# x, residual and output stored block by block; weight conversions in half rows; x ahead of the conditioning weights; weight folding moved away from the gMLP scratch

## What is computed

```python
for l in range(DEPTH):                            # DEPTH = 2
    mod = adaln(c, w_mod[l], b_mod[l])            # 9 x (shift, scale, gate) from SiLU(c) @ w_mod
    mod_c = adaln(c_ctx, w_mod[l], b_mod[l])
    h = ffn_sublayer(h, mod, 0, norm_g[l, 0], ffn_w_gu[l, 0], ffn_w_down[l, 0])
    hc = ffn_sublayer(hc, mod_c, 0, ...)
    xa_c, ga_c, u_c, v_c, f_c = mix_in(hc, mod_c, norm_g[l, 1], w_in[l])
    y_lru_c, state_c = lru_branch(xa_c, ...)      # bidirectional gated scan; context first
    xa, ga, u, v, f = mix_in(h, mod, norm_g[l, 1], w_in[l])
    y_lru, _ = lru_branch(xa, ..., state_c)
    h = mix_out(h, mod, y_lru, ga, u, v, f, gmlp_ws[l], gmlp_bs[l], w_out[l])
    h = ffn_sublayer(h, mod, 6, norm_g[l, 2], ffn_w_gu[l, 1], ffn_w_down[l, 1])
    ...                                           # the same for hc, except in the last layer
return rmsnorm(h, final_norm_g)
```

## Time and profile before

| | |
|---|---|
| median of 3 runs (all) | 5353.59 us (5323.27, 5353.59, 5664.02) |
| profiled execution: time / span of its slowest core | 5341.42 us / 5339.9 us |
| spans of the 8 cores | 5308.5 to 5339.9 us |
| PE busy | 4829.8 us, 90% |
| DVE, ACT, POOL busy | 40%, 30%, 20% |
| granted PE clock, mean | 0.961 to 0.964 of full speed |
| moved by DMA | 893 MB, 167 GB/s |
| plain DMAs (q1) / converting DMAs (q0), share of the 16 DMA engines | 45.9% / 15.0% |

### The profile page before, as it was taken

The page is one execution under the profiler, slowest core; times in us unless marked ns, Lnnn a source line. Parts: engine busy times, 40 slices in busy tenths (PEclk is TensorE's granted clock), DMA queues, the critical chain, the costliest instruction groups (busy, mean ns, idle before and its releaser), DMA issues.

```text
span 5339.9 us, 84731 instructions; the slowest of 8 cores (5308.5 to 5339.9 us)
## 1 busy us (share of the span) xinstructions
PE 4829.8 (90%) x29137; PEld 2772.7 (52%) x29137; DVE 2116.0 (40%) x3151; ACT 1624.3 (30%) x2551; POOL 1062.5 (20%) x943
## 2 busy tenths in 40 slices
PE   4987889999867999989999989999997679999998
PEld 2553556564424565555546546566544235555554
DVE  2325354544453424323222354434445443534422
ACT  2223333423344212212112243433334432322312
POOL 1311121312111211212121220312210131221210
PEclk9998999999988999999999999999998889999999
DMA  8973668786636667577576646556456444444434
GB/s 179 204 176 113 167 177 214 171 197 184 201 130 170 173 180 205 153 179 171 158 209 160 180 139 185 159 155 175 152 177 211 155 134 144 153 132 152 154 114 150
DMA packets 321601, 893.15 MB, mean 167 GB/s; under 512 B 32032, under 2 KB 83616, under 8 KB 320032
## 3 DMA queue, kind: packets, MB, share of 16 engines
q1 hardware_dynamic: 292960, 767.91, 45.9%
q0 software_dynamic: 28224, 119.82, 15.0%
HBM read 861.37 MB, written 204.24 MB: 200 GB/s over the span
## 4 chain that ended last, share of the span: by engine, by line
PE 74%; DMA 8%; DVE 7%; ACT 4%; issue 4%; POOL 2%; SPq 1%; DVEq 0%; ACTq 0%; POOLq 0%
PE ps L937 42%; PE ps L987 19%; PE ps L1545 4%; PE ps L1030 4%; DMA arena<-wgu_s 2%; PE ps L1052 2%; DMA hT<-arena 1%; DVE arena L1277 1%; DVE arena L1273 1%; DVE arena L1281 1%; DVE arena L994 1%; POOL arena L847 1%; DMA arena<-smalls 1%; DVE arena L890 1%; ACT arena L1248 1%
## 5 line engine op out<-in xcount | busy, mean ns | idle before, releaser
L937 PE MATMUL ps<-arena 128*128 128x384 bf16 (+2 forms) x15136 | 2613.5, 334 | 98.7 <-DMA arena<-wgu_s 40.6
L937 PEld LDWEIGHTS ps<-arena 128*128 128x128 bf16 x15136 | 1480.0, 98 | 1185.7 <-issue 137.2
L987 PE MATMUL ps<-arena 128*128 128x384 bf16 (+2 forms) x7568 | 1346.2, 340 | 2.8 <-DVE arena L948 1.1
L948 DVE TENSOR_TENSOR arena<-arena,ps 128x384 bf16<-128x384 bf16 (+2 forms) x946 | 533.5, 568 | 1837.5 <-PE ps L937 1457.8
L987 PEld LDWEIGHTS ps<-arena 128*128 128x128 bf16 x7568 | 753.6, 100 | 569.3 <-issue 57.5
L946 ACT ACTIVATE arena<-ps 128x384 bf16<-128x384 f32 (+2 forms) x946 | 468.9, 500 | 1541.6 <-PE ps L937 1461.9
L847 POOL TENSOR_TENSOR arena<-arena 128x768 f32<-128x768 f32 (+2 forms) x287 | 503.8, 1755 | 2139.4 <-ACT arena L845 2031.7
L845 ACT ACTIVATE arena<-arena 128x768 f32<-128x768 f32 (+1 forms) x287 | 228.2, 795 | 878.3 <-DVE arena L994 516.9
L994 DVE SCALAR_TENSOR_TENSOR arena<-ps,arena 128x384 f32<-128x384 f32 (+2 forms) x344 | 216.1, 630 | 701.7 <-PE ps L987 532.4
L897 POOL TENSOR_SCALAR arena<-arena 128x768 bf16<-128x768 f32 (+2 forms) x252 | 273.0, 1084 | 898.0 <-DVE arena L890 894.0
L890 DVE TENSOR_TENSOR arena<-arena 128x768 f32<-128x768 f32 (+2 forms) x296 | 292.8, 995 | 71.9 <-POOL arena L897 42.7
(11 more groups left out here) (117 smaller groups left out, 2374.0 us busy)
## 6 DMA issues: line engine op xcount, KB each, us to landing
arena<-wgu_s SPq DMA_DIRECT2D x506, 512.0 KB, 4.9
arena<-wdn_s SPq DMA_DIRECT2D x368, 352.0 KB, 3.3
arena<-wmod_h POOLq DMA_DIRECT2D x72, 512.0 KB, 8.2
hT<-arena SPq DMA_DIRECT2D x24, 1536.0 KB, 11.1
arena<-hT SPq DMA_DIRECT2D x24, 1536.0 KB, 14.0
arena<-win_s SPq DMA_DIRECT2D x66, 512.0 KB, 5.4
wgu_s<-wgu_h POOLq DMA_DIRECT2D x66, 512.0 KB, 11.2
arena<-xc_d SPq DMA_DIRECT2D x64, 384.0 KB, 4.9
```

Source lines behind the costliest of these rows:

```text
L937: ins = e.matmul(ps[:, 0:n], ap[:, kc * 256 + u * 128:kc * 256 + u * 128 + 128], NT[nx][:, kc, off:off + n], start=(kc == 0), stop=(kc == ...
L948: P.op("dve", lambda e: e.tensor_tensor(hid[:, j, off:off + n], sg[q][:, 0:n], PS[banks[1]][:, 0:n], ALU.mult), reads=[R_sg[q], R_ps[banks ...
L987: ins = e.matmul(ps[:, 0:n], ap[:, jj * 128:jj * 128 + 128], hid[:, j, off:off + n], start=(j == 0), stop=(j == JC - 1))
```

## The change

Five things change.

- **Layout.** `xT`, `ctxT`, `hT` and `outTb` were [chunk, partition, token]: one block's row of one chunk is a run of 2 or 3 KB. They become flat arrays in which a block is [partition, chunk, token] (`blocked`), so that a half block of 768 tokens is one run of 12 KB per partition, on the SBUF side too. Blocks of 512 tokens and the context (held in slots of 768) keep runs of 2 KB and 1 KB in SBUF. The first block of x is still loaded chunk by chunk.
- **Start.** The load of `mod` tile 0 waits until chunk 5 of x has landed. All 8 `pos_add`/`sq_pe` steps come first, then `rstd_from`, then the 8 `mod` tiles.
- **Conversions.** A `precast` is issued as two half rows: the leading dimension of both sides is 2, where the built program had 16 pieces of 16384 elements (`wgu`, `win`) or 128 rows of 1408 (`wdn`).
- **Statistics.** `stat_step` goes from 0.08 to 0.16 of the first list, the normalisation from 0.2 to 0.24.
- **Folding and CLc.** `fold_out(0)` goes from the third block's pump to the first block's list; `fold_in(1)` and `fold_out(1)` go to the head of the second sweep's pump. The load of `CLc` is issued before `mix_xa` instead of with the context's Fourier step.

```diff
@@ -416,9 +416,16 @@
...
     CS_d = din("CS", [128, 256], BF16)
-    outT = nc.dram_tensor("outTb", [KC, 128, L], F32, kind="ExternalOutput").ap()
-
-    hT = dscr("hT", [KC, 128, NTOK], F32)
+    outB = nc.dram_tensor("outTb", [D * L], F32, kind="ExternalOutput").ap()
+
+    hB = dscr("hB", [D * L], F32)
+    hBc = dscr("hBc", [D * CTX], F32)
+
+    def blocked(t, tok, n):
+
+        a = D * tok
+        return t[a:a + D * n].rearrange("(p m t) -> p m t", p=128, m=KC)
+
     xc_d = dscr("xc_d", [4, 128, NTOK], F32)
@@ -621,7 +628,7 @@
...
             if k == "mod":
-                P.dma("pool", ap, wmod_h[key[1], key[2]], writes=[res], key=res.name)
+                P.dma("pool", ap, wmod_h[key[1], key[2]], reads=([R_h[0][KC - 3]] if t == 0 else []), writes=[res], key=res.name)
             elif k == "c0":
@@ -654,7 +661,8 @@
...
             st["pc"] = (i + 1) % 4
-            P.dma("pool", s, f, writes=[scr(key), R_pc[i]], key=f"pc{i}")
+            P.dma("pool", s.rearrange("p (a b) -> a p b", a=2), f.rearrange("p (a b) -> a p b", a=2),
+                  writes=[scr(key), R_pc[i]], key=f"pc{i}")
@@ -792,12 +800,11 @@
...
                     if src == "x":
-                        ap = ctxT[m0:m1] if s == 1 else xT[m0:m1, :, tok - CTX:tok - CTX + n]
-                        rd = []
+                        t, rd = (ctxB if s == 1 else xB), []
                     else:
-                        ap = hT[m0:m1, :, tok:tok + n]
-                        rd = [R_hT[k] for k in blocks_of(tok, n)]
-                    P.dma("sp", h[slot][:, m0:m1, off:off + n], ap.rearrange("m p t -> p m t"), reads=rd,
+                        t, rd = (hBc if s == 1 else hB), [R_hT[k] for k in blocks_of(tok, n)]
+                    ap = blocked(t, tok - CTX * (1 - s), n)[:, m0:m1, :]
+                    P.dma("sp", h[slot][:, m0:m1, off:off + n], ap, reads=rd,
                           writes=R_h[slot][m0:m1], key=f"hl{slot}{m0}", group=grp)
@@ -808,13 +815,13 @@
...
                         continue
-                    o = P.dma("sp", outT[m0:m1, :, tok - CTX:tok - CTX + n].rearrange("m p t -> p m t"),
-                              h[slot][:, m0:m1, off:off + n], reads=R_h[slot][m0:m1], key=f"os{slot}")
+                    o = P.dma("sp", blocked(outB, tok - CTX, n)[:, m0:m1, :], h[slot][:, m0:m1, off:off + n],
+                              reads=R_h[slot][m0:m1], key=f"os{slot}{m0}")
                     out_stores.append(o)
...
                     continue
-                P.dma("sp", hT[m0:m1, :, tok:tok + n].rearrange("m p t -> p m t"), h[slot][:, m0:m1, off:off + n],
+                P.dma("sp", blocked(hBc if s == 1 else hB, tok - CTX * (1 - s), n)[:, m0:m1, :], h[slot][:, m0:m1, off:off + n],
                       reads=R_h[slot][m0:m1], writes=[R_hT[k] for k in blocks_of(tok, n)], key=f"hs{slot}{m0}", group=grp)
@@ -1480,8 +1487,10 @@
...
+            def tables():
+                P.dma("sp", clc[0], CLc_d, writes=[R_tm], key="clc")
+
             def prep():
-                P.dma("sp", clc[0], CLc_d, writes=[R_tm], key="clc")
                 P.op("dve", lambda e: e.memset(tmp[0][:, 0:256], 0.0), writes=[R_tmp[0]])
@@ -1510,7 +1519,7 @@
...
                 P.dma("sp", ybf[j, :, 0:256], yb[q][:, 0:256], reads=[R_yb[q]], writes=[R_ybf["c"]], key=f"ybs{q}", group="c")
-            return [lambda: (prep(), run(0), run(1))]
+            return [tables, lambda: (prep(), run(0), run(1))]
@@ -1607,11 +1616,12 @@
...
         banks0 = [nb(), nb()]
-        for t in range(8):
-            mods[t]()
+        for t in range(KC):
             pos_add(sb0, 0, t)
...
         rstd_from(sb0, banks0)
+        for t in range(8):
+            mods[t]()
         n1 = 0
@@ -1639,7 +1649,7 @@
...
                 if l == 0 and i == 2:
-                    slow_bg += mod_steps(0, 5, 6) + [lambda: fold_in(1), lambda: fold_out(0), lambda: fold_out(1)]
+                    slow_bg += mod_steps(0, 5, 6)
                     slow_bg += [lambda t=t: precast_wo(0, t) for t in range(4)] + mod_steps(0, 6, 9) + precast_ffn(1)
@@ -1649,8 +1659,8 @@
...
                     late = l == 0 and i == 1
-                    bg1 = [(0.08, lambda: stat_step(prev))]
-                    bg1 += spread(norm_steps(prev, pslot, l, 1, n2, "mix")[1:], 0.72 if late else 0.2, 0.9 if late else 0.8)
+                    bg1 = [(0.16, lambda: stat_step(prev))]
+                    bg1 += spread(norm_steps(prev, pslot, l, 1, n2, "mix")[1:], 0.72 if late else 0.24, 0.9 if late else 0.8)
                     if i == 1:
@@ -1661,6 +1671,9 @@
...
                     rest = mix_rest(prev, l, n2)
+                    cf = ctx_fourier(prev)
+                    if late:
+                        cf[0]()
                     for u in mix_xa(prev, l, n2):
@@ -1669,7 +1682,7 @@
...
                     if l == 0 and prev["ctx"]:
-                        bg2 += [(0.05, ctx_fourier(prev)[0])]
+                        bg2 += [(0.0, cf[1])]
                     if not is_last:
@@ -1697,7 +1710,7 @@
...
                 if l == 0 and i == 0:
-                    bg2 += spread(mod_steps(0, 2, 3), 0.5, 0.95)
+                    bg2 += spread(mod_steps(0, 2, 3) + [lambda: fold_out(0)], 0.5, 0.95)
                 run(units, bg2)
@@ -1801,7 +1814,7 @@
...
                 if l == 0 and i == 0:
-                    slow_bg += mod_steps(1, 0, 9)
+                    slow_bg += [lambda: fold_in(1), lambda: fold_out(1)] + mod_steps(1, 0, 9)
                     slow_bg += [lambda t=t: precast(("wi", 1, t)) for t in range(6)] + precast_ffn(2)
```

16 lines of the change are left out of this document (11 added, 5 removed).

## The result

The change makes the kernel slower. The changed kernel takes 5455.3 us (median of 4 runs, 5451.55 to 5544.52), the kernel before 5342.6 us (median of 4 runs); the ratio is 1.0225 with a 95% interval of 1.0185 to 1.0265, so 2.25% are lost, 113 us between the medians. Predicted were 5285 us with a range of 5230 to 5400: even its upper end is 55 us too low.

What follows compares the result with a forecast made beforehand. The prediction took PE to bound the kernel, except for DMA at the start and in a few short collisions. Its terms, -20 - 7 - 8 - 9 - 15 = -59 us, took 5341.4 to 5282, said as 5285; range 5230 to 5400.

Steps and rivals of the forecast that it cites:

- What bounds the kernel: Whole kernel: PE bounds it, busy 90% of the span, except for DMA at the start and a few short collisions.
- Layout and half rows: Bursts of conversions: halved packets and longer residual runs let SP's queue move more bytes; -15 us, bounds 0 and -25.
- rival a: Conversions spread over few DMA engines, POOL late and PE behind it at the projection: 5380 to 5415 us, chance 0.12.
- The start: Before the first matmuls: PE starts at 60 instead of 86.25 us; -20 us, bounds -8 and -26.
- Folding: gMLP steps: PE's 9.6 us wait for ACT's copies goes once folds move; -8 us, bounds -10 and +6.
- CLc: Table load issued before the projection, whose matmuls cover its landing: PE's 6.9 us wait goes; -7 us, bounds -7 and 0.
- statistics: First-sweep stages: PE waits less for POOL's sum of squares, 28.2 us before; -9 us, bounds 0 and -20.
- The sum: Whole kernel: -20 - 7 - 8 - 9 - 15 = -59 us from 5341.4 gives 5282, said as 5285.
- rival (b): The start gives little and the collisions stay, DMA-bound as far as 300 us: -25 us, 5316, chance 0.23.
- The signs: Right if PE's wgu_s waits fall below 25 us; wrong if wgu_h waits exceed 15 us or the clock drops below 0.96.
- The chances: Whole kernel's time: 0.15 for faster by over 2%, 0.04 for slower by over 2%, 0.81 for within 2%.

Runs made afterwards that it cites:

- e1: The changed kernel with only the conversions undone, each again one DMA of 16 pieces or of 128 rows of 1408: ratio to before 1.000, 5342.8 us profiled.
- e4: The changed kernel with each conversion issued as two DMAs of 128 half rows: ratio to before 0.998, 5331.5 us profiled.
- e6: e4 with all three folds back in the third block's pump, where they were before: 5296.8 us profiled, ratio to before 0.9947 (0.9887 to 1.0007).
- e14: The changed kernel with the folds back in the third block and the conversions as before, in full rows: 5318.1 us profiled, no ratio.
- e12: The kernel before with the blocked layout of x, residual and output alone: ratio to before 1.0009, 5363.3 us profiled.
- e7: The kernel before with only the start changed: ratio to before 0.9968 (0.9931 to 1.0005), 5319.8 us profiled.
- e5: e4 with each of the two folds at the head of the second sweep cut into two pump steps: ratio to before 0.9949, 5310.9 us profiled.
- e9: The changed kernel with conversions as two DMAs of 128 half rows and each fold in two steps back in the third block: 5327.0 us profiled, no ratio.
- e3: The changed kernel with conversions in whole rows, still with a leading dimension of 2: lowest time 5480.5 us, core median +138 us against before, no ratio.
- e11: The changed kernel with conversions in whole rows and a leading dimension of 8 (8 x 16 x 2048): ratio to before 0.997.
- e10: The changed kernel with conversions of leading dimension 16 in short pieces (16 x 128 x 128 for wgu): ratio to before 1.0158, 5438.1 us profiled.
- e13: The changed kernel with wgu or win conversions as 16 x 64 x 256 and half wdn tiles as 16 x 8 x 1408: ratio to before 0.9985.

## Why the prediction was wrong, point by point

- **What bounds the kernel: right, but one view short.** PE is the bound, and DMA is at the start. I read SP's queue only by landing times. Its waits would have shown that SP already stood 26.4 and 6.2 us for conversions: the conversions are consumed by SP's loads soon after they are issued, so that a longer landing goes straight into the queue that all weights come through.
- **Layout and half rows, -15 us (bounds 0 and -25): the step that failed.** It counted the bytes and lengths of packets, and took no effect at all as its worst case; that a conversion could land later, and that SP's loads wait for it, is not in the term. With the leading dimension at 2 the term is about +115 us (core medians: after +113, e1 -3). The unknown was written down (rival a) and left out of the term. "Halving" the packets is also not what the edit did to a `wgu` tile: its pieces went from 16384 elements to 1024. As for the mechanism which the step did argue, that shorter rows let SP's queue through, the runs with a spread conversion agree: -6 to -11 us (e4 against e1) and -21 us (e6 against e14). The layout's share of it was nothing (e12). And the 40.6 us of which 15 were to be won were those of the core with the longest waits; others had 22.5.
- **Rival (a), 0.12, 5380 to 5415 us: right in the cause, wrong in the place and the price.** Landing 22 to 45 us was said, 31.5 measured, above the threshold of 28. But I let POOL be late with the normalisation, and wrote of the burst at 2288 that POOL's idle time until 2380 "hides even 11 us each". POOL's idle time hides nothing, since it is SP that waits for the landing. Just that stage lost most. POOL's late normalisation did not show: PE's waits at L1037 for L904 are 4.1 us. And "the burst then presses less on SP's loads" was true and worthless: a tile's load in the burst landed in 17.5 us instead of 40.1, well inside my sign of "under 25 us", while PE's waits for tiles went from 40.6 to 113.5 us, because landing is counted from the issue, and the issue was what came late.
- **The start, -20 us: right by itself as far as the runs tell** (e7: core median -16, lag -22 at the end), with the first L944 at 64.8 us on core 7, inside 56 to 66, though the hand-over was 4.8 us later than my 60. The eight tiles follow each other by 2.6 to 4.3 us, where I took 3.2, and the last is used at 49.2 instead of 44 to 45; most of PE's 26.8 us for `wmod_h` are waits for these tiles. What failed was that idle DMA time between 86 and 300 us takes up `woutf` and its stores: 12 us were lost at 204 us (e6 against e4), and 4.5 to 9.0 of them are PE behind ACT, which waits for the fold's own store. The term had priced the bytes of those stores and not this wait.
- **Folding, -8 us (-10 and +6): wrong in sign.** It is about +35 us (e4 against e6). That "six PSUM banks cover for two units of about 2.6 us" makes room for some 5 us of waiting for a store; ACT waited 22.3 us for it in the second sweep and 15.9 us in the first block.
- **CLc, -7 us, and statistics, -9 us: right as waits.** The 6.9 us are gone (2.8 us for DVE stand at the same matmuls now), and 28.2 became 15.9 us. That the time fell by as much is not shown, as neither ran alone; together with the layout, on top of the start, they bring 5 us (core medians: e7 -16, e14 -21).
- **The sum.** Start, CLc and statistics add up to -40 us by the waits that went; measured together with full-row conversions and old folds they are -21 (e14). Some of the gain is given back to waits for `wgu_s` tiles, 36 to 41 us there where e7 has 24 to 39. With the folds moved it is about 0 (e1). So the forecast of 5285 us would have failed with a sound form of the conversions too (e4: 5331.5 us profiled): rival (b), -25 us, is nearest to e14, and the folds take the rest.
- **The signs.** PE's waits for `wgu_s` (75.3 us) did not fall below 25. The wait for `wgu_h` tiles between 100 and 200 us was 3.1 us, under the 15 named. The granted clock did fall below the 0.96 of before, to 0.95, and came with the longer waits of PE; which part of the time is its own no run separates.
- **The chances.** 0.04 for slower by over 2% was far too small. That no transfer before had such a dimension was known, and a landing three times as long was written down; a price for it had to be carried to every consumer, SP's loads first.

## What to carry to other kernels

Where a DMA's shape is changed, look first at its outermost dimension, and keep it at 8 or more: here 2 made landing three times as long at the same share of the engines' time, and 8 did not (what lies between was not run). Follow a late transfer to the queue that waits for it, by that queue's own waits; a short landing time says nothing of a load that could not be issued. A step moved off one stall takes the stall with it if its halves share one scratch and wait for each other's store. Splitting the step into halves with other work between them took the wait away here (e5, e9).

## What the hardware showed that was not expected

- **Packets that carry nothing.** e3 has 107520 packets under 512 bytes more than e1 (139552 against 32032) and 0.43 MB more on its converting queue (120.25 against 119.82): 4.0 bytes each. After has 215040 more and 0.86 MB: 4.0 bytes again. Per row of a conversion (120 conversions of 256 or 128 rows) that makes 7 with a leading dimension of 2; with 8 it is 1 (e11: 15360), with 16 none. That is 16 divided by the leading dimension, less one. What they are the traces don't say. They cost little of the engines' time (15.1% in after, 15.0% before).
- **POOL's issue** of a conversion took 0.5 us before, 1.1 us with 2048 packets (after, e10), 0.8 us with 1024 (e3, e13) and 0.6 us with 8 x 16 x 2048 (e11); POOL is busy for 20 to 21% of the span before and after.
- **Short pieces**: with a leading dimension of 16, 2048 pieces of 256 bytes raise the converting queue's share from 15% to 22.3% and cost 1.6% of the time (e10).
